# Attention's blocks by head half: score matmuls of two heads on different array rows back to back, and three steps for the value sums in place of five

## The chip, the cores and the metric

The kernel runs on one core of a Trainium2 chip. The metric is device time in microseconds (us), the median of several runs; less is better. The engines are TensorE (PE; PEld is its weight load), VectorE (DVE), ScalarE (ACT), GpSimd (POOL) and SyncE (SP, which issues the loads of weights). Each engine works through its own instructions in order and waits on semaphores for the others.

## The reference, cut to what matters

Two layers of one model, then two layers of a second one (FFN, mixer, FFN), on 512 tokens of width 1024. Only the mixer of the second model is touched, and in it the banded attention: 8 query heads of 64, 2 key/value heads (each serves 4 query heads), 4 blocks of 128 queries, and each block sees itself and its neighbours (2 or 3 blocks of keys).

```python
scores = einsum("bnqkgd,bnskd->bnkgqs", qb, kb) * HEAD_DIM ** -0.5
scores = where(valid, scores, -1e30)              # |q - k| <= 128
m = maximum(max(scores, -1), sink)
p = exp(scores - m);  denom = sum(p, -1) + exp(sink - m)
o = einsum("bnkgqs,bnskd->bnqkgd", p, vb) / denom
```

Beside attention the mixer has a projection of the input (`w_in`), a gated short convolution (3 taps), a wide convolution (31 taps over 2 x 128 channels, with a layer norm behind it), and a projection by `w_out`.

## The kernel before, in words

Each engine has a class (`TensorE`, `VectorE`, `ScalarE`, `Pool`) with one Python generator for each part of the work. A `yield` is a step; `mix(main, side, main_steps, side_steps)` (line 185) lays the steps of two generators beside each other in that ratio, the same way on each engine, so the order of the instructions on an engine is fixed by where the generators yield. In the mixer (`mixer`, TensorE line 1047, VectorE line 1945, ScalarE line 2531) the main generator is `attention` with 80 steps and the side generator is `beside` with 78: one side step is one three-part matmul (`three`, lines 576 to 578: each product of two numbers split in a high and a low half takes three 512-column passes) of the other projections, and for VectorE one tap of the wide convolution (`wide_conv`, line 1234 with `acc`; 60 in all, 16 of them before attention) and, every few steps, the making of a low half of a weight unit (`wlo`), whose high half ScalarE makes (`whi`, line 2161).

`BLOCKS` lists the eight blocks of attention: query block `nb` and key head `kvh`, so that each block holds the four query heads of one key head. I call them B0 to B7. For each block:

- `scores` (TensorE line 1182): for each of four heads one fp32 matmul of 64 rows (the head's 64 numbers) by 256 or 384 keys into one PSUM bank, then a step. The rows are 0 to 63 for key head 0 and 64 to 127 for key head 1, so all four of a block lie on the same rows. VectorE adds the mask and takes the maximum (line 2118) from the bank into `pr`, which frees the bank; behind the fourth come three small operations on `sm`. In the second block of a query block, `turn_ao` turns the finished outputs of the query block before (behind the third head's scores); ScalarE and VectorE copy them out in `copy_ao` and `lower_ao` (`xh`, `xl`).
- `weights` (ScalarE line 2661): four exponentials with row sums, and one of the sink.
- `values` (TensorE line 1193), one block behind the scores: `turned(i)` transposes a head's weights in 2 or 3 pieces of 128 (line 582), ScalarE copies them to `prT` (line 2683, three buffers), and line 1214 multiplies them with the values in pairs of 64-column halves of the array. The order is turned 0 and 1, step, head 0 and turned 2, step, head 1 and turned 3, step, head 2, step, head 3, step. VectorE then divides by the sums (`ao`).

A block thus takes 4 + 1 steps for scores and 5 for values, 80 in all. Scores, turned weights and turned outputs take their PSUM banks in turn from four (`self.ps`), in the last two blocks from three (`self.ps3`); a bank is taken again only when the engine that reads it is done. Elsewhere too matmuls use part of the array's rows: `grams` (line 996) issues four 64-row matmuls that go in turn to rows 0 to 63 and 64 to 127, each pair in two banks (line 1002).

Of the kernel before, what the change touches and what calls it, by code (L numbers as in the profile page):

```python
# [11 lines left out]
ALU = mybir.AluOpType  # L12
# [363 lines left out]
SIDE = (337, 321)  # L376
LEVELS = tuple(enumerate((2, 4, 8, 16, 32, 64)))
OUT_ROWS = (0, 768, 256, 512)
BLOCKS = tuple((nb, kvh, max(nb - 1, 0), min(nb + 2, 4) - max(nb - 1, 0)) for nb in range(4) for kvh in range(2))


class Lane:
# [153 lines left out]
class TensorE(Lane):  # L536
# [510 lines left out]
    def mixer(self, l):  # L1047
        k = self.k
        st = ("mix", l)
        self.at(st)  # L1050
        units = [self.coming("w_in_2", (l,), tuple((256 * u + 128 * j, 768 + 64 * h, 64) for j in range(2) for h in QHEADS))
                 for u in range(4)]
        for t, u in ((2 * tp + t, 2 * up + u) for tp in range(2) for up in range(2) for t in range(2) for u in range(2)):
            wh, wl, i = units[u]
            bank = k.bank(("q", l, t)) if u else self.bank(self.all4, ("q", l, t))
            self.wait_ge(("hi", i), ("lo", i), ("hh", st, t, u // 2), ("hl", st, t, u // 2))
            for j in range(2):
                d = 2 * u + j
                x = slice(512 * d + 128 * t, 512 * d + 128 * t + 128)
                a = self.three(bank[:, :], k.hh[:, x], k.hl[:, x], HALF(wh, j), HALF(wl, j), d == 0, d == 7)  # L1060
            a.then_inc(*self.up(*([("used", i)] if t == 3 else []), *([("q", l, t)] if u == 3 else [])))
            if t < 2 and (t, u) in ((1, 1), (1, 2)):
                self.to_hT_tile(st, 1 + u)
            elif t == 3 and u in (1, 3):
                self.turn_q(l, u // 2)
        for n, _ in enumerate(self.conv_pair(l, 0), 1):
            if n % 8 == 0:
                self.turn_q(l, 1 + n // 8)
        units = [self.coming("w_in_2", (l,), tuple((512 * u + 128 * j, 1280, 256) for j in range(4))) for u in range(2)]
        for t in range(4):  # L1070
# [12 lines left out]
        side = self.beside(l)  # L1083
        for n in range(6):
            next(side)
            if n % 3 == 2:
                self.turn_k(l, n // 3)
        self.at(("pj", st))
        mix(self.attention(l), side, 80, 78)
        drain(side)  # L1090
        keys = [("pj", st, 1, t) for t in range(4)]
        for n, _ in enumerate(self.tiles(keys, "w_out_2", (l,), OUT_ROWS, 512, k.xh8, k.xl8, lambda d: (), self.last4, 4)):
            if n in (9, 11):
                self.to_hT_tile(("ffn2", l), n // 11, self.spare4)
        self.all4.n = 0
# [83 lines left out]
        self.wait_ge(("aon", l, nb, 1))  # L1179
        self.turn(bank, [k.ao[:, i * 128:(i + 1) * 128] for i in range(4)], ("aot", l, nb))  # L1180

    def scores(self, l, nb, kvh, k0, nk):
        k = self.k
        for i in range(4):
            h, q = 4 * kvh + i, 64 * kvh
            bank = self.bank(self.rows_rota, ("as", l, nb, h))
            self.wait_ge(("qT", l, nb), ("kT", l, (k0 + nk - 1) // 2))
            self.e.matmul(bank[:, 0:nk * 128], k.qT[q:q + 64, i * 512 + nb * 128:i * 512 + (nb + 1) * 128],  # L1188
                          k.kT[q:q + 64, k0 * 128:(k0 + nk) * 128], start=True, stop=True).then_inc(*self.up(("as", l, nb, h)))
            if i == 2 and kvh and nb:  # L1190
                self.turn_ao(l, nb - 1)
            yield

    def values(self, l, nb, kvh, k0, nk):
        k = self.k
        at = (l, nb, kvh)
        n0 = 4 * (2 * nb + kvh)
        out = self.bank(self.ao1, ("ao", at))

        def turned(i):  # L1200
# [5 lines left out]
        turned(0)  # L1206
        turned(1)
        yield
        for i in range(4):
            h = 4 * kvh + i  # L1210
            pT = k.prT[(n0 + i) % 3]
            self.wait_ge(("aT", at, i), ("vv", l, (k0 + nk - 1) // 2))
            for j, r in itertools.product(range(nk), (0, 64)):
                t = self.e.matmul(out[r:r + 64, h * 64:(h + 1) * 64], pT[:, j * 128 + r:j * 128 + r + 64],  # L1214
                                  k.v2[:, (k0 + j) * 128 + kvh * 64:(k0 + j) * 128 + kvh * 64 + 64], start=j == 0,
                                  stop=j == nk - 1, skip_group_check=True)
            t.then_inc(*(self.up(("av", at, i), ("ao", at)) if i == 3 else self.up(("av", at, i))))
            if i < 2:
                turned(i + 2)
            yield  # L1220


class VectorE(Lane):
# [721 lines left out]
    def mixer(self, l):  # L1945
# [23 lines left out]
        side = self.beside(l)  # L1969
# [1 line left out]
            next(side)  # L1971
        self.at(("pj", st))
        self.paced = True
        mix(self.attention(l), side, 80, 78)
        drain(side)
        self.paced = False
        self.project(4, st, ("ffn2", l), ALPHA, "ln2", 1e-5, self.held)
# [129 lines left out]
        self.lower(v8(k.xl8), k.bank(key)[:, :].rearrange("p (j n) -> p j n", j=4), v8(k.xh8), [("xah", l, nb)],  # L2107
                   [("free", key)] + ([("xl", l, j) for j in range(2, 6)] if nb == 3 else []))

    def scores(self, l, nb, kvh, k0, nk):  # L2110
        k = self.k
        n0 = 4 * (2 * nb + kvh)
        mo = (k0 - nb + 1) * 128
        s = k.sm[(2 * nb + kvh) % 2]
        for i in range(4):
            key = ("as", l, nb, 4 * kvh + i)
            self.wait_ge(key, ("amask", l), *([("at", (l, nb - 1, kvh), 3)] if nb else []))
            self.e.tensor_tensor_reduce(k.pr[(n0 + i) % 8][:, 0:nk * 128], k.bank(key)[:, 0:nk * 128], k.amask[:, mo:mo + nk * 128],
                                        1.0, -3e38, ALU.add, ALU.max, s[:, i:i + 1]).then_inc(*self.up(("free", key)))
            yield  # L2120
        sk = k.sink[:, 4 * kvh:4 * kvh + 4]
        self.wait_ge(("sink", l))
        self.stt(s[:, 0:4], s[:, 0:4], 0.125, sk, ALU.mult, ALU.max).then_inc(*self.up())
        self.wait_ge()
        self.ts(s[:, 4:8], s[:, 0:4], -1.0, None, ALU.mult).then_inc(*self.up())
        self.wait_ge()
        self.tt(s[:, 8:12], sk, s[:, 0:4], ALU.subtract).then_inc(*self.up(("asm", (l, nb, kvh))))

    def weights(self, l, nb, kvh, k0, nk):
        s = self.k.sm[(2 * nb + kvh) % 2]  # L2130
        self.wait_ge(("ape", (l, nb, kvh)))
# [4 lines left out]
    def values(self, l, nb, kvh, k0, nk):  # L2136
        k = self.k
        at = (l, nb, kvh)
        s = k.sm[(2 * nb + kvh) % 2]
        for i in range(5):  # L2140
            if i == 3:
                self.weights(l, nb, kvh, k0, nk)
            yield
        o = slice(kvh * 256, kvh * 256 + 256)
        self.wait_ge(("ao", at), *([("aot", l, nb - 1)] if nb and kvh == 0 else []))
        self.tt(k.ao[:, o].rearrange("p (h n) -> p h n", h=4), k.bank(("ao", at))[:, o].rearrange("p (h n) -> p h n", h=4),
                s[:, 16:20].unsqueeze(2).broadcast_to([128, 4, 64]), ALU.mult).then_inc(
            *self.up(("aon", l, nb, kvh), ("free", ("ao", at))))


class ScalarE(Lane):
# [379 lines left out]
    def mixer(self, l):  # L2531
# [26 lines left out]
        side = self.beside(l)  # L2558
# [3 lines left out]
                self.turned_k(l, n // 3)  # L2562
        self.at(("pj", st))
        self.paced = True
        mix(self.attention(l), side, 80, 78)
        drain(side)
        self.paced = False
        self.project(4, st, ("ffn2", l), self.held)
# [69 lines left out]
    def attention(self, l):  # L2638
        held = None
        for at in BLOCKS:  # L2640
            for _ in range(4):
                yield
            if at[1] and at[0]:
                self.copy_ao(l, at[0] - 1)
# [16 lines left out]
    def weights(self, l, nb, kvh, k0, nk):  # L2661
        k = self.k
        at = (l, nb, kvh)
        n0 = 4 * (2 * nb + kvh)
        s = k.sm[(2 * nb + kvh) % 2]
        self.wait_ge(("asm", at))
        for i in range(4):
            x = k.pr[(n0 + i) % 8][:, 0:nk * 128]
# [2 lines left out]
        self.wait_ge()  # L2671
        self.act(s[:, 8:12], s[:, 8:12], ACT.Exp).then_inc(*self.up(("ape", at)))

    def values(self, l, nb, kvh, k0, nk):
        k = self.k
        at = (l, nb, kvh)
        n0 = 4 * (2 * nb + kvh)

        def turned(i):
            g, u = divmod(n0 + i - 3, 4)  # L2680
# [5 lines left out]
        turned(0)  # L2686
        turned(1)
        yield
        for i in range(4):
            if i < 2:  # L2690
                turned(i + 2)
            yield


class Pool(Lane):
# [272 lines left out]
```

## Time and profile before

| | us |
|---|---|
| median of 3 runs | 3395.89 (3393.03 to 3396.45) |
| the profiled execution | 3399.57 |
| its span, first to last instruction | 3397.8 |
| PE busy in the span | 3248.0 (96%) |
| DVE busy | 1725.3 (51%) |
| ACT busy | 1097.9 (32%) |
| POOL busy | 155.7 (5%) |
| mean granted TensorE clock | 0.988 |

The span is what the profile's rows add up to; the execution's own time has 1.8 us around it. A busy PE is not PE at its peak, as matmuls overlap: what a group of matmuls costs is read from the starts of the rows around it. Attention of the first layer lies from 1913 to 2042 us, that of the second from 2865 to 2995 us.

### The profile page before, as it was taken

The page shows a single profiled execution, that of the slowest core. Times are in us where ns is not written, and L with a number is a line of the kernel's source. Part 1 is how long each engine was busy: PE and PEld are TensorE (multiplying, and loading weights), DVE is VectorE, ACT ScalarE, POOL GpSimd, SP SyncE. Part 2 cuts the span into 40 slices and gives each one's busy share as a digit, 9 for nine tenths or more (in the row PEclk, how much of TensorE's full clock was granted, in tenths as well). Part 3 has the DMA queues.
Part 4 walks back from the last instruction along what each step waited for, and adds up shares of the span by engine and source line. Part 5 has one row for each costly group of instructions (what it writes and reads, how often), then busy time and mean ns, then how long its engine had stood idle before and what let it go on. Part 6 is the DMA issues. An engine that isn't in the chain of part 4 may idle for free. (4 is left out here: it accounts for less than half of the span.)

```text
span 3397.8 us, 52042 instructions
## 1 busy us (share of the span) xinstructions
PE 3248.0 (96%) x21576; PEld 2552.2 (75%) x21576; DVE 1725.3 (51%) x2526; ACT 1097.9 (32%) x1615; POOL 155.7 (5%) x204
## 2 busy tenths in 40 slices
PE   6999899989999999999999999999999999999998
PEld 5776666767776677788888658888888886588887
DVE  6655654456546644553325866333433347763324
ACT  4342233324433333332322343232233223433321
POOL 1000100000000000000001000000000000000000
PEclk9999899999999999999999999999999999999999
DMA  6222122222222111222232212223222322122232
GB/s 230 76 87 98 67 75 88 94 85 94 88 82 73 63 45 58 97 96 99 95 110 93 81 38 87 99 93 112 87 100 97 109 80 100 39 80 93 100 112 75
DMA packets 83531, 303.74 MB, mean 89 GB/s; under 512 B 9680, under 2 KB 9952, under 8 KB 83296
## 3 DMA queue, kind: packets, MB, share of 16 engines
q1 hardware_dynamic: 78064, 283.11, 23.7%
q0 software_dynamic: 5232, 17.31, 1.5%
q8 instruction: 170, 2.79, 0.3%
q14 instruction: 65, 0.53, 0.0%
HBM read 295.66 MB, written 4.72 MB: 88 GB/s over the span
## 5 line engine op out<-in xcount | busy, mean ns | idle before, releaser
L576 PE MATMUL bank<-hh,whi 128*128 128x512 f32 (+1 forms) x2704 | 1075.9, 398 | 27.3 <-DVE hl L1228 9.5
L578 PE MATMUL bank<-hh,wlo 128*128 128x512 f32 (+1 forms) x2704 | 1027.6, 380 | 0.0
L577 PE MATMUL bank<-hl,whi 128*128 128x512 f32 (+1 forms) x2704 | 1027.2, 380 | 0.0
L1228 DVE TENSOR_TENSOR wlo<-raw,whi 128x1024 fp32r<-128x1024 f32 x498 | 610.5, 1226 | 730.4 <-ACT whi L2161 681.2
L2161 ACT CAST whi<-raw 128x1024 fp32r<-128x1024 f32 x498 | 523.6, 1051 | 733.7 <-PE bank L578 668.2
L576 PEld LDWEIGHTS bank<-hh,whi 128*128 128x128 f32 x2704 | 512.8, 190 | 167.1 <-issue 50.5
L578 PEld LDWEIGHTS bank<-hh,wlo 128*128 128x128 f32 x2704 | 513.0, 190 | 97.7
L577 PEld LDWEIGHTS bank<-hl,whi 128*128 128x128 f32 x2704 | 514.3, 190 | 80.6 <-issue 2.5
L576 PE MATMUL bank<-whi,fh 128*128 128x512 f32 x704 | 274.4, 390 | 0.0
L578 PE MATMUL bank<-whi,fl 128*128 128x512 f32 x704 | 273.9, 389 | 0.0
L577 PE MATMUL bank<-wlo,fh 128*128 128x512 f32 x704 | 273.9, 389 | 0.0
L1228 DVE TENSOR_TENSOR tmp<-tmp,bank 128x512 f32<-128x512 f32 x104 | 71.6, 688 | 240.5 <-PE bank L578 238.1
L2510 ACT CAST fh<-tmp 128x512 fp32r<-128x512 f32 x88 | 54.5, 619 | 374.9 <-DVE tmp L1228 374.9
L578 PEld LDWEIGHTS bank<-whi,fl 128*128 128x128 f32 x704 | 132.1, 188 | 27.6
L577 PEld LDWEIGHTS bank<-wlo,fh 128*128 128x128 f32 x704 | 132.2, 188 | 27.2
L576 PEld LDWEIGHTS bank<-whi,fh 128*128 128x128 f32 x704 | 132.1, 188 | 27.2
L1228 DVE TENSOR_TENSOR fl<-tmp,fh 128x512 fp32r<-128x512 f32 x88 | 61.0, 694 | 71.3 <-ACT fh L2510 71.3
L2429 ACT COPY X<-bank 128x256 f32<-128x256 f32 x96 | 35.8, 373 | 178.1 <-PE bank L582 177.2
L1234 DVE SCALAR_TENSOR_TENSOR acc<-ccp,cols,acc 128x512 f32<-128x512 f32 x120 | 90.2, 752 | 4.3
L576 PE MATMUL bank<-oh,whi 128*128 128x512 f32 x192 | 81.8, 426 | 7.9 <-DVE ogs L1228 7.9
L2156 ACT ACTIVATE tmp<-bank 128x512 f32<-128x512 f32 x120 | 72.0, 600 | 52.0 <-PE bank L578 48.8
L1757 DVE COPY_PREDICATED U<-lmask,bank 128x256 f32<-128x256 uint32 x64 | 32.7, 510 | 99.4 <-PE bank L902 94.1
(325 smaller groups left out, 3488.7 us busy)
## 6 DMA issues: line engine op xcount, KB each, us to landing
raw<-in_W SPq DMA_DIRECT2D x514, 512.0 KB, 3.2
bc<-in_ln_g POOLq DMA_DIRECT2D x6, 512.0 KB, 4.2
bc<-in_ln_b POOLq DMA_DIRECT2D x6, 512.0 KB, 5.8
xn<-in_x SPq DMA_DIRECT2D x4, 512.0 KB, 9.1
mrg<-in_W SPq DMA_DIRECT2D x2, 1024.0 KB, 13.0
AR<-in_W SPq DMA_DIRECT2D x2, 1024.0 KB, 18.4
xn<-in_x POOLq DMA_DIRECT2D x4, 512.0 KB, 4.9
xd<-xn POOLq DMA_DIRECT2D x4, 512.0 KB, 3.5
```

Source lines behind the costliest of these rows:

```text
L576: e.matmul(out, ah, bh, start=first, stop=False, skip_group_check=True)
L577: e.matmul(out, ah, bl, start=False, stop=False, skip_group_check=True)
L578: return e.matmul(out, al, bh, start=False, stop=last, skip_group_check=True)
L1228: return self.e.tensor_tensor(o, a, b, op)
L1234: return self.e.scalar_tensor_tensor(out=o, in0=a, scalar=s, in1=b, op0=op0, op1=op1)
L1757: e.copy_predicated(FOUR_PART(U, 1, n), m, TIGHT(wb, n)).then_inc(*self.up(("cu", at, lv + 1), ("free", ("cw", at, lv))))
L2156: return self.e.activation(o, a, f, bias=bias, scale=scale, **kw)
L2161: self.e.copy(self.k.halves(i)[0], self.k.raw_unit(n)).then_inc(*self.up(("hi", i)))
L2429: self.e.copy(TIGHT(X, n), FOUR_PART(k.bank(key), 0, n)).then_inc(*self.up(("cx", at, lv), ("free", key)))
L2510: self.e.copy(HALF(k.fh, m), tm).then_inc(*self.up(("fh", st, m)))
```

## The change

The two key heads share a block now, and two heads of each make up its four: block half 0 has heads 0, 4, 1, 5 and half 1 has heads 2, 6, 3, 7. Neighbours in this order lie on rows 0 to 63 and 64 to 127. Scores yield once for two heads; in `values`, heads 0 and 1 follow each other, then turned 2 and 3, a step, heads 2 and 3, a step. So a block takes 2 + 1 steps for scores and 3 for values, 48 in all, and `mix` lays 78 side steps beside 48. `turn_ao` comes behind the fourth head's scores. The views of VectorE's small operations and of `ao` follow the new order of heads.

```diff
-BLOCKS = tuple((nb, kvh, max(nb - 1, 0), min(nb + 2, 4) - max(nb - 1, 0)) for nb in range(4) for kvh in range(2))
+BLOCKS = tuple((nb, half, max(nb - 1, 0), min(nb + 2, 4) - max(nb - 1, 0)) for nb in range(4) for half in range(2))
+HEADS = tuple(tuple((a, v, 4 * v + a) for a in (2 * half, 2 * half + 1) for v in range(2)) for half in range(2))
+BY_HALF = lambda x, half: x.rearrange("p (v a n) -> p a v n", v=2, a=4)[:, 2 * half:2 * half + 2, :, :]
+BY_PAIR = lambda x: x.rearrange("p (a v) -> p a v", v=2)
...
-        mix(self.attention(l), side, 80, 78)
+        mix(self.attention(l), side, 48, 78)
...
     (TensorE)
-    def scores(self, l, nb, kvh, k0, nk):
-        for i in range(4):
-            h, q = 4 * kvh + i, 64 * kvh
+    def scores(self, l, nb, half, k0, nk):
+        for i, (a, v, h) in enumerate(HEADS[half]):
+            q = 64 * v
             bank = self.bank(self.rows_rota, ("as", l, nb, h))
...
-            if i == 2 and kvh and nb:
+            if i == 3 and half and nb:
                 self.turn_ao(l, nb - 1)
-            yield
+            if i % 2:
+                yield
...
-        for i in range(4):
-            h = 4 * kvh + i
+        for i, (_, v, h) in enumerate(HEADS[half]):
             pT = k.prT[(n0 + i) % 3]
             self.wait_ge(("aT", at, i), ("vv", l, (k0 + nk - 1) // 2))
             for j, r in itertools.product(range(nk), (0, 64)):
...
-            if i < 2:
-                turned(i + 2)
-            yield
+            if i == 1:
+                turned(2)
+                turned(3)
+            if i % 2:
+                yield
...
     (VectorE)
+            if i % 2:
+                yield
-        sk = k.sink[:, 4 * kvh:4 * kvh + 4]
+        sk = k.sink[:, :].rearrange("p (v a) -> p a v", v=2)[:, 2 * half:2 * half + 2, :]
...
-        for i in range(5):
-            if i == 3:
-                self.weights(l, nb, kvh, k0, nk)
+        for i in range(3):
+            if i == 2:
+                self.weights(l, nb, half, k0, nk)
             yield
...
-        self.tt(k.ao[:, o].rearrange("p (h n) -> p h n", h=4), k.bank(("ao", at))[:, o].rearrange("p (h n) -> p h n", h=4),
-                s[:, 16:20].unsqueeze(2).broadcast_to([128, 4, 64]), ALU.mult).then_inc(
+        self.tt(BY_HALF(k.ao[:, :], half), BY_HALF(k.bank(("ao", at))[:, :], half),
+                BY_PAIR(s[:, 16:20]).unsqueeze(3).broadcast_to([128, 2, 2, 64]), ALU.mult).then_inc(
...
     (ScalarE, attention)
-            for _ in range(4):
+            for _ in range(2):
                 yield
...
     (ScalarE, values)
-        for i in range(4):
-            if i < 2:
-                turned(i + 2)
-            yield
+        turned(2)
+        turned(3)
+        yield
+        yield
```

## Rows read from the trace of the kernel before

**Rows 1.** Stretches of attention: length, busy of each engine (instructions), PEclk, DMA, GB/s.
```profile
1913.00:1966.80 53.80, 49.06 (x249) 28.59 (x249) 50.60 (x102) 21.39 (x50) 1.06 (x2) 0.94 0.19 65
1966.80:1985.10 18.30, 18.00 (x129) 11.23 (x128) 14.09 (x29) 7.65 (x17) 0.00 (x0) 0.99 0.08 30
1985.10:2042.40 57.30, 53.76 (x349) 33.10 (x347) 29.07 (x66) 31.28 (x67) 0.00 (x0) 1.00 0.10 38
1961.00:1967.00 6.00, 5.27 (x28) 3.65 (x30) 5.53 (x9) 1.73 (x5) 0.00 (x0) 0.50 0.07 29
```

**Rows 2.** Waits in 1913 to 2043 (PE), 1913 to 1985 (DVE): total, times, longest.
```profile
PE bank L582 <- DVE xl L1228: 5.6, 3, 3.9
...
DVE ao L1228 <- PE bank L1214: 2.9, 2, 2.3
DVE tz L1228 <- PE bank L578: 0.5, 1, 0.5
```

**Rows 3.** PE by time: its longest wait's end; then a head's scores, 384 keys.
```profile
1961.73 0.47 PE L582 MATMUL bank<-ident,pr 128*128 128x128 f32 x1 [3.86 <-DVE xl L1228]
...
1970.17 0.40 PE L578 MATMUL bank<-hh,wlo 128*128 128x512 f32 x1
1970.49 0.91 PE L1188 MATMUL bank<-kT,qT 64*128 64x384 f32 x2
1971.33 0.50 PE L576 MATMUL bank<-hh,whi 128*128 128x512 f32 x1
1971.67 0.40 PE L577 MATMUL bank<-hl,whi 128*128 128x512 f32 x1
1971.90 0.40 PE L578 MATMUL bank<-hh,wlo 128*128 128x512 f32 x1
```

**Rows 4.** The same around scores of 256 keys.
```profile
1915.82 0.40 PE L578 MATMUL bank<-hh,wlo 128*128 128x512 f32 x1
1916.14 0.70 PE L1188 MATMUL bank<-kT,qT 64*128 64x256 f32 x2
1916.77 0.50 PE L576 MATMUL bank<-hh,whi 128*128 128x512 f32 x1
1917.11 0.39 PE L577 MATMUL bank<-hl,whi 128*128 128x512 f32 x1
```

**Rows 5.** PE at line 1002, four matmuls in turn on both halves of the rows.
```profile
270.30 0.49 PE L1002 MATMUL bank<-AR,KH 64*128 64x256 f32 x2
...
270.30 1.14 PE L1002 MATMUL bank<-AR,KH 64*128 64x256 f32 x8
271.36 0.50 PE L576 MATMUL bank<-whi,hh 128*128 128x512 f32 x1
```

**Rows 6.** PE, value sums: head with turned weights; head alone; a head of two key blocks.
```profile
1979.80 0.40 PE L578 MATMUL bank<-hh,wlo 128*128 128x512 f32 x1
...
1981.24 0.40 PE L577 MATMUL bank<-hl,whi 128*128 128x512 f32 x1
...
1982.87 0.39 PE L578 MATMUL bank<-hh,wlo 128*128 128x512 f32 x1
1983.19 0.57 PE L1214 MATMUL bank<-v,prT 128*64 128x64 f32 x12
1984.03 0.40 PE L577 MATMUL bank<-hl,whi 128*128 128x512 f32 x1
...
2040.89 0.45 PE L1214 MATMUL bank<-v,prT 128*64 128x64 f32 x8
```

**Rows 7.** DVE in order of time: the last tap, and what follows it.
```profile
1984.34 0.75 DVE L1234 SCALAR_TENSOR_TENSOR acc<-ccp,cols,acc 128x512 f32<-128x512 f32 x1
1986.35 0.56 DVE L2118 CUSTOM_DVE_ANT_0 pr<-bank,amask 128x384 f32<-128x384 f32 x1 [1.26 <-PE bank L1188]
```

**Rows 8.** ACT in order of time, B5's last copies to B6's first.
```profile
2016.63 0.99 ACT L2683 COPY prT<-bank 128x384 f32<-128x384 f32 x2
2027.55 0.37 ACT L2683 COPY prT<-bank 128x256 f32<-128x256 f32 x1
```

More of the change, by code:

```diff
@@ L1180, in turn_ao, with values @@
         self.turn(bank, [k.ao[:, i * 128:(i + 1) * 128] for i in range(4)], ("aot", l, nb))
-    def scores(self, l, nb, kvh, k0, nk):
+    def scores(self, l, nb, half, k0, nk):
         k = self.k
-        for i in range(4):
-            h, q = 4 * kvh + i, 64 * kvh
+        for i, (a, v, h) in enumerate(HEADS[half]):
+            q = 64 * v
             bank = self.bank(self.rows_rota, ("as", l, nb, h))
             self.wait_ge(("qT", l, nb), ("kT", l, (k0 + nk - 1) // 2))
-            self.e.matmul(bank[:, 0:nk * 128], k.qT[q:q + 64, i * 512 + nb * 128:i * 512 + (nb + 1) * 128],
+            self.e.matmul(bank[:, 0:nk * 128], k.qT[q:q + 64, a * 512 + nb * 128:a * 512 + (nb + 1) * 128],
                           k.kT[q:q + 64, k0 * 128:(k0 + nk) * 128], start=True, stop=True).then_inc(*self.up(("as", l, nb, h)))
-            if i == 2 and kvh and nb:
+            if i == 3 and half and nb:
                 self.turn_ao(l, nb - 1)
-            yield
-    def values(self, l, nb, kvh, k0, nk):
+            if i % 2:
+                yield
+    def values(self, l, nb, half, k0, nk):
         k = self.k
-        at = (l, nb, kvh)
-        n0 = 4 * (2 * nb + kvh)
+        at = (l, nb, half)
+        n0 = 4 * (2 * nb + half)
         out = self.bank(self.ao1, ("ao", at))
@@ L1214, in values @@
                 t = self.e.matmul(out[r:r + 64, h * 64:(h + 1) * 64], pT[:, j * 128 + r:j * 128 + r + 64],
-                                  k.v2[:, (k0 + j) * 128 + kvh * 64:(k0 + j) * 128 + kvh * 64 + 64], start=j == 0,
+                                  k.v2[:, (k0 + j) * 128 + v * 64:(k0 + j) * 128 + v * 64 + 64], start=j == 0,
                                   stop=j == nk - 1, skip_group_check=True)
             t.then_inc(*(self.up(("av", at, i), ("ao", at)) if i == 3 else self.up(("av", at, i))))
-            if i < 2:
-                turned(i + 2)
-            yield
+            if i == 1:
[3 more added lines that the diff above has]
+                yield
 class VectorE(Lane):
@@ L1973, in mixer @@
         self.paced = True
-        mix(self.attention(l), side, 80, 78)
+        mix(self.attention(l), side, 48, 78)
         drain(side)
@@ L2108, in lower_ao, with scores @@
                    [("free", key)] + ([("xl", l, j) for j in range(2, 6)] if nb == 3 else []))
-    def scores(self, l, nb, kvh, k0, nk):
+    def scores(self, l, nb, half, k0, nk):
         k = self.k
-        n0 = 4 * (2 * nb + kvh)
+        n0 = 4 * (2 * nb + half)
         mo = (k0 - nb + 1) * 128
-        s = k.sm[(2 * nb + kvh) % 2]
-        for i in range(4):
-            key = ("as", l, nb, 4 * kvh + i)
-            self.wait_ge(key, ("amask", l), *([("at", (l, nb - 1, kvh), 3)] if nb else []))
+        s = k.sm[(2 * nb + half) % 2]
+        for i, (_, _, h) in enumerate(HEADS[half]):
+            key = ("as", l, nb, h)
+            self.wait_ge(key, ("amask", l), *([("at", (l, nb - 1, half), 3)] if nb else []))
             self.e.tensor_tensor_reduce(k.pr[(n0 + i) % 8][:, 0:nk * 128], k.bank(key)[:, 0:nk * 128], k.amask[:, mo:mo + nk * 128],
                                         1.0, -3e38, ALU.add, ALU.max, s[:, i:i + 1]).then_inc(*self.up(("free", key)))
-            yield
-        sk = k.sink[:, 4 * kvh:4 * kvh + 4]
+            if i % 2:
+                yield
+        sk = k.sink[:, :].rearrange("p (v a) -> p a v", v=2)[:, 2 * half:2 * half + 2, :]
         self.wait_ge(("sink", l))
-        self.stt(s[:, 0:4], s[:, 0:4], 0.125, sk, ALU.mult, ALU.max).then_inc(*self.up())
+        self.stt(BY_PAIR(s[:, 0:4]), BY_PAIR(s[:, 0:4]), 0.125, sk, ALU.mult, ALU.max).then_inc(*self.up())
         self.wait_ge()
@@ L2126, in scores, with weights @@
         self.wait_ge()
[L2127 to L2131, printed above, removed]
+        self.tt(BY_PAIR(s[:, 8:12]), sk, BY_PAIR(s[:, 0:4]), ALU.subtract).then_inc(*self.up(("asm", (l, nb, half))))
+    def weights(self, l, nb, half, k0, nk):
+        s = self.k.sm[(2 * nb + half) % 2]
+        self.wait_ge(("ape", (l, nb, half)))
         self.tt(s[:, 8:12], s[:, 8:12], s[:, 12:16], ALU.add).then_inc(*self.up())
@@ L2134, in weights, with values @@
         self.e.reciprocal(s[:, 16:20], s[:, 8:12]).then_inc(*self.up())
-    def values(self, l, nb, kvh, k0, nk):
+    def values(self, l, nb, half, k0, nk):
         k = self.k
-        at = (l, nb, kvh)
-        s = k.sm[(2 * nb + kvh) % 2]
-        for i in range(5):
-            if i == 3:
-                self.weights(l, nb, kvh, k0, nk)
-            yield
-        o = slice(kvh * 256, kvh * 256 + 256)
-        self.wait_ge(("ao", at), *([("aot", l, nb - 1)] if nb and kvh == 0 else []))
-        self.tt(k.ao[:, o].rearrange("p (h n) -> p h n", h=4), k.bank(("ao", at))[:, o].rearrange("p (h n) -> p h n", h=4),
-                s[:, 16:20].unsqueeze(2).broadcast_to([128, 4, 64]), ALU.mult).then_inc(
-            *self.up(("aon", l, nb, kvh), ("free", ("ao", at))))
+        at = (l, nb, half)
+        s = k.sm[(2 * nb + half) % 2]
+        for i in range(3):
+            if i == 2:
+                self.weights(l, nb, half, k0, nk)
+            yield
+        self.wait_ge(("ao", at), *([("aot", l, nb - 1)] if nb and half == 0 else []))
+        self.tt(BY_HALF(k.ao[:, :], half), BY_HALF(k.bank(("ao", at))[:, :], half),
+                BY_PAIR(s[:, 16:20]).unsqueeze(3).broadcast_to([128, 2, 2, 64]), ALU.mult).then_inc(
+            *self.up(("aon", l, nb, half), ("free", ("ao", at))))
 class ScalarE(Lane):
@@ L2564, in mixer @@
         self.paced = True
-        mix(self.attention(l), side, 80, 78)
+        mix(self.attention(l), side, 48, 78)
         drain(side)
@@ L2659, in copy_ao, with weights @@
             *self.up(("xah", l, nb), *([("xh", l, j) for j in range(2, 6)] if nb == 3 else [])))
-    def weights(self, l, nb, kvh, k0, nk):
+    def weights(self, l, nb, half, k0, nk):
         k = self.k
-        at = (l, nb, kvh)
-        n0 = 4 * (2 * nb + kvh)
-        s = k.sm[(2 * nb + kvh) % 2]
+        at = (l, nb, half)
+        n0 = 4 * (2 * nb + half)
+        s = k.sm[(2 * nb + half) % 2]
         self.wait_ge(("asm", at))
@@ L2672, in weights, with values @@
         self.act(s[:, 8:12], s[:, 8:12], ACT.Exp).then_inc(*self.up(("ape", at)))
-    def values(self, l, nb, kvh, k0, nk):
+    def values(self, l, nb, half, k0, nk):
         k = self.k
-        at = (l, nb, kvh)
-        n0 = 4 * (2 * nb + kvh)
+        at = (l, nb, half)
+        n0 = 4 * (2 * nb + half)
         def turned(i):
@@ L2688, in values @@
         yield
-        for i in range(4):
-            if i < 2:
-                turned(i + 2)
-            yield
+        turned(2)
+        turned(3)
+        yield
+        yield
 class Pool(Lane):
```

## The prediction, made before the change was run

> **What bounds the kernel now.** I read the page first: PE is busy for 96% of the span, DVE for half of it. So what shortens PE shortens the kernel, unless another engine holds PE up in that stretch. Next the table of stretches over attention in the first layer, where the change lies, since the average over the span says nothing about it [rows 1]. The second layer shows the same picture 952 us later, with the same waits to 0.3 us, so I work out one layer and double it. The reader is to see three things.
>
> First, from 1913 to 1966.8 us DVE is busy for 50.60 of 53.80 us with 102 instructions; the 3.2 us left are 0.03 us between one and the next, and no wait of DVE falls in it. DVE is full there: PE hands it scores, and it has the taps of the wide convolution besides. PE is idle for 4.7 us in the same stretch. Second, from 1966.8 to 1985.1, where the last tap ends [rows 7], DVE waits for 3.4 us in all, 2.9 of it for the value sums and 0.5 for a bank of the short convolution [rows 2]. Those 2.9 us come from PE's own wait of 3.9 us for a bank that DVE frees in `lower_ao` (`xl`), after which PE ran at a granted clock of 0.50 (1.2 GHz) for 6 us [rows 1 to 3]. Third, from 1985.1 to 2042.4 PE is busy for 53.76 of 57.30 us and DVE for 29.07: PE is the bound, with 3.5 us of gaps.
>
> **Scores.** A full pass of 512 columns starts 0.23 us after the one before (1971.67 to 1971.90) [rows 3]. From the pass ahead of a head's scores to the second pass behind them it takes 1.50 us with 384 keys; two passes would take 0.46, so these scores cost 1.04 us, of which 0.84 is from their start to the next start. With 256 keys it is 1.29 - 0.46 = 0.83, with 0.63 from start to start [rows 4]. The difference of the starts, 0.21 us for 128 keys, gives 0.42 us for the streaming of 256 keys, and the rest is a fixed cost at each change from full matmuls to these and back. The old code lays a side step between any two heads, so each head pays it.
>
> Do two heads on different rows really run at the same time? Line 1002 answers it in this trace: four matmuls of 64 rows by 256 columns, in turn on the upper and the lower rows, two banks. The first passes of the first two start together (two are there within 0.02 us), and the four take 1.06 us to the next start [rows 5]. One after another they would take 0.63 + 3 x 0.42 = 1.89; as two pairs side by side 0.63 + 0.42 = 1.05. The new score pairs have the same form: rows 0 to 63 and 64 to 127, each into its own bank. So a pair costs what a head cost, and one of each two heads is free: 16 pairs in a layer, 8 with 384 keys and 8 with 256, 8 x 1.04 + 8 x 0.83 = 15.0 us of PE. The bounds: nothing side by side leaves the fixed cost saved, about 0.2 us a pair (1.04 - 0.84), 3.2 us; above 15.0 I see nothing.
>
> **Value sums.** A head alone costs 1.16 - 0.46 = 0.70 us; with turned weights behind it 1.44 - 0.46 = 0.98 [rows 6]. Its 12 matmuls show 0.57 us against 0.45 for 8, which is 0.06 us for each pair of halves, so a head directly behind another adds 6 x 0.06 = 0.36 in place of 0.70. The change joins heads 0 and 1, and 2 and 3: 2 x 0.34 = 0.68 us a block, 5.4 us in 8 blocks. The lower bound is 0.2 a joint (entry 0.09 and exit 0.11 against 0.23), 3.2 us. Turned 2 and 3 together save nothing I can see: three pieces alone cost 0.28 behind a head and stream for longer than they wait.
>
> Together PE loses 20.4 us of work in a layer. What of it reaches the end differs by stretch.
>
> **Stretch one, to the last tap.** The 78 side steps stay, and the last tap (the 44th of attention's side steps) still falls behind B4: 45 x 78/80 before, 27 x 78/48 after. In it PE saves 4 x 0.83 + 6 x 1.04 + 4 x 0.68 = 12.3 us, but DVE's work is the same: the same reductions, the same taps, small operations of the same 4 columns in another view, the same 256 elements of `ao` (0.42 us each; a few hundredths either way at most). DVE can only lose its 3.4 us of waits. Will it? PE gets further ahead, stops sooner for banks, and is at hand when DVE frees one. The one wait that matters is again for `xl`, now before turned 3 only, as `turn_ao` comes one bank later. Behind it PE owes turned 3, two joined heads, three groups of side steps (4.9 x 0.69) and one pair of scores, some 5.7 us, before DVE runs dry: released at 1961.73 [rows 3], PE had DVE at work until 1966.8 [rows 1], 5.1 us, to which come `ao` (0.4), 1.6 taps at 0.75 [rows 7] and one multiply (0.7), 7.4 us. At the full clock that covers it. But PE will again have stood for some 4 us, and if the clock falls again for 6 us [rows 1] the 5.7 become 8.7 and DVE waits 1.3. I take 2.5 of the 3.4 us, with bounds 0 and 4.7 (the 1.3 us more if PE is already past the scores for which DVE waits right behind the last tap [rows 7]).
>
> **Stretch two, PE bound.** Here PE saves two pairs at 1.04 and four at 0.83, 5.4 us, and four blocks of value sums, 2.7: 8.1 us. Against it stand two new waits. ACT has no gap from its copies for B5 to the end of the first copy for B6, 2017.62 to 2027.92, 10.3 us (table loads, the wide convolution's SiLU, four exponentials, a cast) [rows 8]. PE's way between the value sums on both sides was 11.8 us and will be 1.06 + 5 x 1.625 x 0.69 + 2 x 0.83 + about 0.9 for the turns = 9.2 us, so it waits about 1.1 us. And in B6 and B7, with three banks, the second pair's second score needs the bank of the first, and turned 0 and 1 come right after two scores in place of one; for these I put 1.0 us, an estimate between 0 and 4 (each of the four turns behind DVE's 0.4 us reductions plus one low half of a unit). Head 1 now waits for its copy directly behind head 0, with turned 2 and 3 queued behind; PE comes there 1.6 side steps after the turn in place of one, so I count nothing (bound 0.3 a block, 1.2 us). Stretch two gives 6.0 us, bounds 3 and 8.1.
>
> The loads and the halving of weights keep their order and place by side step; no DMA moves past another.
>
> **Sum.** 2 x (2.5 + 6.0) = 17 us. The profiled execution took 3399.57, 1.8 over its span, so the changed one is expected at 3382.6. The median of the three runs lies 3.7 lower: 3395.9 - 17 = 3379.
>
> **The rivals.** *DVE takes the whole first stretch.* Nothing comes from it, and only 2 x 6.0 = 12 us are left: 3384. For it: DVE is full for 54 us, and PE's stop for `xl` stays. Against: DVE did wait, and for a PE that now has less to do. The Trainium skill (TensorEngine Tiling (Array Packing), PSUM Bottleneck) says that tiling speeds up TensorE but not the evacuation of PSUM, which may become the bottleneck; the trace has that state already in stretch one and not in stretch two, and by the rule alone this rival would hold.
>
> *The pairs don't overlap.* Then only joints are saved, 0.2 x 6 + 2.7 in stretch two less 1 for waits, and 2 in stretch one: 2 x 4.9, about 3386. Against it stands line 1002.
>
> *All PE work counts.* 2 x 20.4 = 41 us, 3355. Against it a DVE that can't be shortened below 68.7 us in stretch one.
>
> *The other side: the clock.* PE will stand for some 14 us in stretch one of each layer where it stood for 4.7, and each spell of 6 us at 1.2 GHz takes 3 us of PE's work. A spell behind which DVE still has work costs nothing; one that reaches the end of stretch one or lies in stretch two costs its 3 us. It decides from six such spells more in the two layers, which eat the 17 us; with eight the time would be 3395.9 + 7 = 3403. For it: the fall after the 3.9 us wait in both layers. Against: the many shorter waits in the stretch brought no fall. The skill (TensorE: Matmul & The Clock Gate, What's actually happening) states that the throttled clock is the default and that activity releases it; the trace agrees as far as that one wait goes.
>
> **How the numbers follow.** My forecast holds with 0.60, DVE taking all with 0.18, no overlap 0.07, all of PE's work 0.03, the clock 0.05, and 0.07 for waits that leave between 0 and 6 us. The low end takes 4.0 of stretch one's 4.7, the whole 8.1, and 1.4 of stretch two's old gaps of 3.5, which joined steps may close: 2 x 13.5, 3369; the high end 2 x 3 us: 3390. A measurement tells a difference from about 0.2%, 6.8 us, so the same is 3389.1 to 3402.7: faster 0.86, same 0.09, slower 0.05.
>
> **What would show it.** Right: at line 1188 four matmul records start in two pairs within some 0.01 us, and 0.84 us from the first to the next full pass; attention's length, 129.3 us from 1913 to the last `turn_ao`, falls to about 121; DVE has under 2 us of waits to the last tap, and PE some 14 us of idle time there. Wrong: score records of a pair that follow each other by 0.4 us or more; DVE waits of over 3 us in stretch one; a PEclk under 0.9 in stretch two; or PE gaps over 6 us in stretch two, which would put the loss on ScalarE's chain or the three banks.

## The result, and the profile after

The changed kernel takes 3370.57 us (median of 4 runs, 3367.75 to 3373.48) against 3396.17 of the kernel before, measured beside it: ratio 0.9924, 95% interval 0.9909 to 0.9940. On another chip it took 3369.93 against 3397.89, ratio 0.9920 (0.9907 to 0.9934). So the change gives 26 to 28 us where I had forecast 17. The time is within the stated range, near its low end, and some of that is luck: two terms of the sum were too small, as the last part shows, and a kernel without any overlap of heads (E3) took nearly the same time.

The profiled execution took 3367.75 with a span of 3365.9, 31.9 us under the span before. Not all of that belongs to the change: attention begins 4.5 us earlier, at 1908.6, though all code ahead of it is the same. Part of the cause is where the clock fell in those stages: ahead of attention TensorE stood at 1.2 GHz for 51.2 us in this trace and for 58.0 in that of the kernel before, which accounts for at most 3.4 of the 4.5 us; the rest is open. Attention itself, from the first scores to the last `turn_ao`, takes 115.9 us in place of 129.2, the same in both layers: 13.3 us twice. Line numbers have moved: scores are line 1191, value sums 1217, transposes 585, `sm` 2123, and a side step's three passes are 579 to 581.

First the price list. Rows of PE around a pair of scores of 384 keys. The first line counts only the matmuls that start before 1959.70, which are the first passes of the two heads; they start 0.007 us apart. The other lines give the pair whole, in order of time:

```profile
1959.32 0.59 PE L1191 MATMUL bank<-kT,qT 64*128 64x384 f32 x2
...
1959.00 0.39 PE L581 MATMUL bank<-hh,wlo 128*128 128x512 f32 x1
1959.32 0.92 PE L1191 MATMUL bank<-kT,qT 64*128 64x384 f32 x4
1960.16 0.50 PE L579 MATMUL bank<-hh,whi 128*128 128x512 f32 x1
1960.50 0.39 PE L580 MATMUL bank<-hl,whi 128*128 128x512 f32 x1
```

The reader is to compare with [rows 3]: two heads take 0.84 us from start to next start, as one did, and 1960.50 - 1959.00 - 0.46 = 1.04 us with entry and exit. Both signs that I had named for this are there: the four passes of a pair start in two pairs within 0.01 us, and the next full pass starts 0.84 us after the first. A joined pair of value sums with three key blocks costs 1.05 us (forecast 1.06), and with the turned weights behind it 1.66 (0.98 twice before).

Next the stretches. I cut at the first mean matmul of the wide convolution (line 1152, now 1155), which waits for the last tap; the columns are those of [rows 1]. Before:

```profile
1913.10:1988.70 75.60, 70.67 (x387) 41.60 (x388) 66.82 (x134) 31.99 (x74) 1.06 (x2) 0.95 0.16 53
1988.70:2042.40 53.70, 50.16 (x338) 31.33 (x336) 26.84 (x63) 28.24 (x58) 0.00 (x0) 1.00 0.11 40
```

After:

```profile
1908.60:1977.30 68.70, 58.06 (x386) 38.25 (x386) 64.57 (x130) 32.01 (x74) 1.06 (x2) 0.98 0.17 58
1977.30:2024.50 47.20, 44.83 (x337) 31.69 (x337) 29.08 (x66) 28.25 (x58) 0.00 (x0) 0.96 0.13 46
```

VectorE has no wait at all left before the last tap, and PE is idle for 10.6 of 68.7 us. The two rows that decide are PE's at the mean matmul and VectorE's at the last tap:

```profile
1977.33 1.98 PE L1155 MATMUL bank<-acc,mean 128*128 128x512 f32 x4 [1.58 <-DVE acc L1239]
```

```profile
1976.52 0.75 DVE L1239 SCALAR_TENSOR_TENSOR acc<-ccp,cols,acc 128x512 f32<-128x512 f32 x1
```

Before, PE came to this matmul 3.6 us after the last tap had ended (1988.67 against 1985.09). Now it stands there 1.6 us ahead of it. PE's waits after the change, from 1908 to 1978, then from 1977 to 2025 (total, times, longest):

```profile
PE bank L585 <- DVE sm L2123: 4.9, 3, 2.4
PE bank L585 <- ACT pr L2161: 2.3, 1, 2.3
PE bank L1155 <- DVE acc L1239: 1.6, 1, 1.6
PE bank L585 <- DVE xl L1233: 1.3, 1, 1.3
...
PE bank L1217 <- ACT prT L2688: 2.3, 1, 2.3
```

### The profile page after: what moved, and what is told of

It is laid out like the page before. It is cut to its first block and busy times, and to the rows that moved or that the text cites. A ratio compares the mean times of both kernels' runs of the same rounds, so it can differ in the third digit from the quotient of the medians.

```text
span 3365.9 us, 52046 instructions
## 1 busy us (share of the span) xinstructions
PE 3209.7 (95%) x21576; PEld 2544.7 (76%) x21576; DVE 1724.8 (51%) x2526; ACT 1098.0 (33%) x1615; POOL 155.8 (5%) x204
## 5 line engine op out<-in xcount | busy, mean ns | idle before, releaser
L2515 ACT CAST fh<-tmp 128x512 fp32r<-128x512 f32 x88 | 54.5, 619 | 375.2 <-DVE tmp L1233 375.2
```

The costliest lines, as they stand in the source:

```text
L2515: self.e.copy(HALF(k.fh, m), tm).then_inc(*self.up(("fh", st, m)))
```

## The experiments

All timed runs stand beside the kernel before on their own chip. For the traces I give attention's two parts, from the first scores to the mean matmul and from there to the last `turn_ao`; before they are 75.5 and 53.7 us, after 68.7 and 47.1. The parts hold the same work in all kernels but E1, E2, E6 and E9, where the mean matmul stands at another place between the blocks.

**E1, pairs of scores, but the sums in five steps.**

```diff
-        mix(self.attention(l), side, 48, 78)
+        mix(self.attention(l), side, 64, 78)
...
-            if i == 1:
-                turned(2)
-                turned(3)
-            if i % 2:
-                yield
+            if i < 2:
+                turned(i + 2)
+            yield
```

> The changed blocks with scores in pairs on different rows, but the value sums in the old five steps (64 steps of attention beside 78). Theory, PE ahead at the last tap: VectorE's floor of 68.7 us to the last tap stays, and PE reaches the mean matmul of the wide convolution right behind it, 6.8 us earlier than before; behind it only the pairs count, 1 x 1.04 + 4 x 0.83 = 4.4 us. So 11.2 us a layer less about 0.5 of waits: 21 us faster than before, 5 slower than the changed kernel. Rival, the coarser steps themselves gave what the forecast missed: the surplus of the change (26 measured against 17) goes with the steps, and this gives about 12 to 14 us. Rival, all PE work counts: 30 us.

Measured: 3379.76 against 3396.07, ratio 0.9950 (0.9938 to 0.9963), 16 us faster. Parts: 73.1 and 50.1 us in the first layer, 70.5 and 49.2 in the second. The median lies between the first two expectations, and the interval, 13 to 21 us, rules out neither. VectorE's floor of 68.7 does not hold for this order: the last tap and the mean matmul come behind one more pair of scores, so VectorE has two more reductions ahead of its last tap, at 0.6 us each. In the second layer, where it has no wait, it needs 69.9 us to the last tap; in the first it needs 71.6, with 1.8 us of waits for PE. PE was held once for 2.6 us in this part, in both layers, for copies of ScalarE, which had stood itself for a product of VectorE, with a cast still to do. PE, then ScalarE:

```profile
1964.99 0.91 PE L1217 MATMUL bank<-v,prT 128*64 128x64 f32 x12 [2.60 <-ACT prT L2686]
```

```profile
1962.69 0.62 ACT L2620 CAST xh<-tz 128x512 fp32r<-128x512 f32 x1 [7.60 <-DVE tz L1231]
1963.38 1.04 ACT L2164 CAST whi<-raw 128x1024 fp32r<-128x1024 f32 x1
1964.46 0.99 ACT L2686 COPY prT<-bank 128x384 f32<-128x384 f32 x2
```

The clock fell to 1.2 GHz at this wait for 6.8 us, and once more for as long in the second part of that layer. The layers run the same code, yet attention is 6.0 us shorter than before in the first and 9.6 in the second. At 1.2 GHz TensorE stood for 17.1 us of the first and 10.2 of the second, and at half speed the 6.8 us between them are 3.4 us of work, about the size of the difference.

**E2, old blocks and scores, sums in three steps.** The edit is the change's own in `values` on all three engines, with `mix(..., 64, 78)`.

> The old blocks (four heads of one key group) and old scores with a step each, with only the value sums in three steps (64 steps of attention beside 78). Theory: the joints of heads save 0.68 us a block; 2.7 us come in stretch two, and in stretch one between 2.7 and 4 us, since PE gets some of the way ahead of VectorE: 5.4 to 6.7 us a layer, 11 to 13 us in all. Rival, coarser steps gave the surplus: 14 us or more. Rival, the sums wait for ScalarE's copies and save nothing: under 5 us.

Measured: 3391.25 against 3396.07, ratio 0.9988 (0.9979 to 0.9997), 5 us faster, less than I expected (the interval is 1 to 7 us), and within the last rival's "under 5 us". In the traces attention is 2.4 and 4.3 us shorter. Its first parts take 71.4 and 69.9 us, its second 55.5 and 54.9; but here scores of two heads, 2.1 us of PE, lie behind the mean matmul that lay ahead of it before. Set right by that, the first parts gain 2.1 and 3.5 us, and the second only 0.3 and 0.8 of the 2.7 that their joints save. PE's waits in the second part of the first layer, 4.1 us where there were 3.5 before:

```profile
PE bank L582 <- DVE xl L1230: 2.0, 1, 2.0
PE bank L1214 <- ACT prT L2685: 1.8, 1, 1.8
PE bank L582 <- DVE sm L2120: 0.3, 1, 0.3
```

With 64 steps each step has 1.22 side steps beside it in place of 1.6. The sums have then 3.7 side steps to cover their copies, and before they had 4.9. That this is the cause is argued from the waits and not shown; I did not vary the ratio alone. E1 and E2 together give 21 us, and the whole change 26 to 28: the parts do not simply add, as each comes with its own mix.

**E3, the new steps with the old blocks: no two scores side by side.** The kernel before, with

```diff
-        mix(self.attention(l), side, 80, 78)
+        mix(self.attention(l), side, 48, 78)
...
-            if i == 2 and kvh and nb:
+            if i == 3 and kvh and nb:
                 self.turn_ao(l, nb - 1)
-            yield
+            if i % 2:
+                yield
```

and the sums in three steps.

> The changed steps (48 beside 78), scores two after each other and sums in three steps, but the old blocks: all four heads of a block lie on the same rows, so no two scores can run side by side. Theory: a joined pair of scores saves only its 0.2 us of entry and exit, so 16 x 0.2 + 5.4 = 8.6 us of PE a layer in place of 20.4; of it 1 + 2.7 us behind the mean matmul, and 4 to 6.8 ahead of it: 8 to 10 us a layer, 16 to 20 us faster than before and 7 to 10 slower than the changed kernel. The score records of a pair start 0.4 us and more apart. Rival, the rows don't matter: the same time as the changed kernel, 26 us faster than before.

Measured: 3372.15 against 3396.07, ratio 0.9929 (0.9917 to 0.9942), 24 us faster. I was wrong by 4 to 8 us, and the rival had the time right: without any overlap the kernel is as fast as the changed one, within what the intervals tell. But the rows do matter to PE. A pair in this kernel:

```profile
1961.68 0.39 PE L578 MATMUL bank<-hh,wlo 128*128 128x512 f32 x1
1962.00 1.55 PE L1188 MATMUL bank<-kT,qT 64*128 64x384 f32 x4
1963.49 0.50 PE L576 MATMUL bank<-hh,whi 128*128 128x512 f32 x1
1963.82 0.40 PE L577 MATMUL bank<-hl,whi 128*128 128x512 f32 x1
```

It costs 1963.82 - 1961.68 - 0.46 = 1.68 us against 1.04. Overlap is worth 0.64 us a pair, and 0.41 with 256 keys. And joining two scores without overlap saves 2 x 1.04 - 1.68 = 0.40 us, twice what I had put. The parts say where overlap went: the first takes 68.7 us here too, the floor of VectorE, with PE busy for more of it. The second is 1.1 us longer than in the changed kernel in the first layer, and 1.6 in the second, of the 2.3 us that overlap is worth there (one pair at 0.64, four at 0.41):

```profile
1911.30:1980.00 68.70, 63.08 (x386) 41.19 (x386) 64.56 (x131) 32.01 (x74) 1.06 (x2) 1.00 0.18 59
1980.00:2028.20 48.20, 45.63 (x335) 32.49 (x336) 29.06 (x66) 28.24 (x58) 0.00 (x0) 1.00 0.14 45
```

**E4, E5 and E7, VectorE relieved.** In each kernel every second tap is left out, so that the wide convolution is not computed in full:

```diff
             for w in range(1, 31):
-                self.wait_ge()
-                self.stt(ac, cp[:, j, w:w + 512], ...
+                if w % 2 == 0:
+                    self.wait_ge()
+                    self.stt(ac, cp[:, j, w:w + 512], ...
                 yield
```

E4 is the kernel before with that edit, E5 the changed one, E7 the kernel of E3.

> The kernel before without every second tap of the wide convolution (30 of its 60 three-operand instructions on VectorE a layer; that part of the output is left out). The step order is unchanged, so only VectorE's load falls, by 22 x 0.79 = 17 us a layer in stretch one. Theory: before the change PE lost to VectorE only its 4.7 us of waits there and some 3 us of half clock behind them; without them attention takes about 122 us in place of 129: 12 to 16 us faster than the kernel before. Rival, VectorE's load is no bound: no change.

> The changed kernel without the same taps. Theory: with VectorE's floor gone PE's 20.4 us of saved work a layer count nearly whole, less about 3 us for copies of ScalarE: attention takes 104 to 106 us, and the time is 33 to 37 us below that of the kernel before with half taps. Rival, banks and ScalarE's chain bound stretch one of the changed kernel as much as VectorE's amount of work does: 20 to 27 us below, as with all taps.

> The new steps with four heads of one key group in a block (no two scores side by side), without the same taps. Overlap itself is worth 1.68 - 1.05 = 0.63 us a pair with 384 keys and 1.25 - 0.84 = 0.41 with 256, 8.3 us of PE a layer. Theory: with VectorE's floor gone these count: 14 to 17 us slower than the changed kernel with half taps. Rival, overlap is off the path in any case (the two kernels with all taps differed by under 2 us): within 4 us of it.

Measured on one chip, beside 3397.89 of the kernel before:

| | us | ratio to before (95%) | parts of attention, first layer |
|---|---|---|---|
| E4, before | 3382.84 | 0.9956 (0.9944 to 0.9969) | 69.5 + 53.7 |
| E5, after | 3339.88 | 0.9832 (0.9819 to 0.9846) | 54.5 + 47.1 |
| E7, same rows | 3358.18 | 0.9883 (0.9870 to 0.9897) | 60.7 + 48.8 |

E4 is 15 us faster than before, as expected. E5 lies 43.0 us below E4 (21.6 a layer in the traces): all of PE's 40.8 us of saved work count once VectorE is no bound, and two more, as its waits are shorter too, 2.8 us in the first layer against 5.8. E7 lies 18.3 us above E5, against 2 x 8.3 of overlap priced from the rows and 14 to 17 expected; in the traces attention differs by 7.9 and 7.3 us, so 3 of the 18.3 lie outside attention or between executions. The first parts of E5 and E7 show PE without a gap:

```profile
1911.70:1966.20 54.50, 54.46 (x386) 37.66 (x387) 46.93 (x109) 30.77 (x70) 1.06 (x2) 1.00 0.21 73
```

```profile
1911.50:1972.20 60.70, 60.69 (x387) 41.64 (x388) 47.55 (x110) 31.38 (x72) 1.06 (x2) 1.00 0.20 65
```

So the rival of banks and ScalarE's chain is out for stretch one: nothing but VectorE's amount of work holds the changed kernel there. For stretch two it is not: E5's second part takes 47.1 us, the same as with all taps. In E4 and E5 I left out the same 30 instructions, so the difference between them is the change's own; that the relief is worth 30 us to the changed kernel (3369.93 to 3339.88) and 15 to the one before shows how much more the changed kernel leans on VectorE.

**The changed kernel again.**

> The changed kernel once more, on the chip of these runs. 0.9924 of the kernel before, 24 to 28 us faster; attention 115.9 us in both layers unless the clock falls at other places.

Measured: 3369.93, ratio 0.9920 (0.9907 to 0.9934), attention 115.9 us in both layers.

**E6, taps spread over 54 side steps in place of 50.**

```diff
-            want = min(10 + m, 60) + sum(m >= x for x in self.norm_steps)
+            want = min(10 + m * 50 // 54, 60) + sum(m >= x for x in self.norm_steps)
-    norm_steps = (52, 58)                      # TensorE
+    norm_steps = (56, 61)
-    norm_steps = (54, 60, 63, 64, 66, 71)      # VectorE
+    norm_steps = (58, 63, 65, 66, 68, 72)
-    norm_steps = (55, 61, 68)                  # ScalarE
+    norm_steps = (59, 64, 70)
```

> The changed kernel with the wide convolution's 50 taps of the side steps spread over 54 of them in place of 50, and the mean, variance and norm behind them 1 to 4 side steps later (they still end before the output projection wants them). Theory: VectorE is the floor up to the last tap, while PE stands for some 10 us; with the last tap 4 side steps later, PE has done 4 x 0.69 = 2.8 us more when the taps end, and nothing of VectorE's own work grows, so 2 to 2.8 us a layer, 4 to 5.5 us faster than the changed kernel, 30 us faster than before. Rival, PE is bound in stretch one by the banks and not by VectorE's amount of work: no change against the changed kernel, or slower by what the squeezed norm makes the output projection wait.

> The changed kernel with its taps spread over 54 side steps once more, on the chip of the two above, since its gain over the changed kernel (4.3 us of attention in the trace) is near what a measurement can tell. 0.9905 to 0.992 of the kernel before; attention 113.7 us in both layers.

Measured: 3366.93 against 3396.07, ratio 0.9913 (0.9899 to 0.9926), and again 3366.27 against 3397.01, ratio 0.9912 (0.9899 to 0.9926). The medians lie 3 to 4 us below those of the changed kernel, and the traces say 115.9 - 113.7 = 2.2 us of attention in each of both layers, the same in two executions. That is the size that the theory gave, but the trace does not show its path: PE still stands for 10.0 us in the first part (10.6 before this edit), and what went is most of its wait for ScalarE's copies, 2.6 to 0.9 us in the layer, and the fall of the clock behind it. The edit moves taps and norm together, and I did not separate them. As the intervals of the ratios overlap, the trace carries this claim more than the times do. It is the fastest full kernel of the study. Its parts:

```profile
1913.20:1988.10 74.90, 64.91 (x443) 43.48 (x444) 69.27 (x143) 34.48 (x79) 1.06 (x2) 0.98 0.18 61
1988.10:2027.00 38.90, 37.38 (x282) 25.92 (x280) 24.33 (x53) 27.05 (x55) 0.00 (x0) 1.00 0.12 41
```

**E8, low halves on GpSimd, and E9, both edits.** Within attention VectorE leaves out the subtraction for `wlo`, and GpSimd does it:

```diff
     def halve(self, i, n):                      # VectorE
+        if self.lend is not None:
+            self.lend.append((i, n))
+            return
...
+        for i, n in k.lent[l]:                  # Pool, mixer
+            hi, lo = k.halves(i)
+            self.wait_raw(n)
+            self.wait_ge(("hi", i), *([("used", i - RING)] if i >= RING else []))
+            self.e.tensor_tensor(lo, k.raw_unit(n), hi.bitcast(F32), ALU.subtract).then_inc(*self.up(("lo", i)))
```

> The changed kernel with the low halves of the weight units that fall into attention made by GpSimd in place of VectorE (one subtraction of 1024 columns each, 1.23 us on VectorE, five of them in stretch one). Theory: VectorE's floor to the last tap falls by 5 x 1.26 = 6.3 us, PE stands for 10 us there now, so 5 to 6 us a layer, 10 to 12 us faster than the changed kernel, if GpSimd makes each half in under the 5.5 us that a unit's eight side steps take. Rival, GpSimd is slow or holds VectorE up: PE waits for the low halves, and the time is that of the changed kernel or worse.

> Both edits: the taps spread over 54 side steps and the low halves on GpSimd. Theory: PE's 10 us of waits in stretch one fall to 2 or less; 5 to 8 us a layer, 10 to 16 us faster than the changed kernel, so about 3357. Rival, GpSimd as above: no faster than the spread taps alone, 3366.

Measured: E8 3380.52, ratio 0.9955 (0.9942 to 0.9967), some 10 us slower than the changed kernel; E9 3371.18, ratio 0.9928 (0.9914 to 0.9941), 5 slower than E6. The rival holds by VectorE being held up; PE does not wait for the low halves. A GpSimd subtraction and VectorE at the same time, in E8:

```profile
1945.63 2.86 POOL L2865 TENSOR_TENSOR wlo<-raw,whi 128x1024 fp32r<-128x1024 f32 x1 [8.51 <-PE bank L586]
```

```profile
1945.49 0.75 DVE L1241 SCALAR_TENSOR_TENSOR acc<-ccp,cols,acc 128x512 f32<-128x512 f32 x1
1946.28 2.23 DVE L1241 SCALAR_TENSOR_TENSOR sm<-sm,sink 128x4 f32<-128x4 f32 x1
1948.54 0.17 DVE L1238 TENSOR_SCALAR sm<-sm 128x4 f32<-128x4 f32 x1
```

An operation on four columns takes 2.23 us in place of 0.16 and ends 0.02 us behind GpSimd's. The taps from 1908 to 1985 come to 0.90 us in the mean, 0.75 without GpSimd:

```profile
L1241 DVE SCALAR_TENSOR_TENSOR acc<-ccp,cols,acc 128x512 f32<-128x512 f32 x52 | 46.8, 901 | 1.9
L1241 DVE SCALAR_TENSOR_TENSOR sm<-sm,sink 128x4 f32<-128x4 f32 x5 | 2.9, 578 | 0.2
```

52 x 0.15 + 5 x 0.42 = 9.9 us are lost where five halves of 1.23 us are saved, and the first part grows from 68.7 to 73.0. The Trainium skill states it (SBUF — State Buffer, SBUF: two separate sides): the ports that VectorE and GpSimd share are an exclusive lock for a whole instruction, also against a VectorE operation with two SBUF inputs. The trace agrees in both forms seen here, and with the `sm` operation to 0.02 us.

## Why the prediction was right, and where it was short

**Prices.** Right, nearly to the hundredth: pair 1.04, joined sums 1.05, 0.6 to 0.7 a block at the joints. That line 1002 already had the answer on overlap holds. One bound was wrong: I took the fixed cost of scores as 1.04 - 0.84 = 0.20 us, but the 0.84 from start to next start holds another 0.2 besides its 0.64 of streaming. E3's rows give 0.40. In the rival without overlap it would have made 16 x 0.2 = 3.2 us more PE work saved in a layer, which takes that rival from 3386 to 3380 at most. E3 was 24 us faster than before, and 3380 is 16: what is still missing is the handover below, which that rival left out as my forecast did.

**Stretch one's floor.** Right: with this order and all its work VectorE needs 68.7 us to the last tap; 68.65 and 68.67 were measured in the two layers of the changed kernel, 68.64 and 68.66 in E3, with no wait of VectorE in either. I had taken 2.5 of the 3.4 us (3.3 came), for fear of the clock behind the wait for `xl`. That wait was 1.3 us this time, as PE had lost time in earlier waits (for `sm` and `pr`), and the clock did not fall there.

**The handover.** This is the term that was mis-sized most. A layer gave 13.3 us where I had 8.5, and of the 4.8 between them about 2.5 are the handover, 1.4 the balance of waits in stretch two, and 0.8 the waits of VectorE that I had kept. I split the gain at the last tap and gave stretch two only PE's savings behind it, 8.1 us less 2.0 for new waits; 10.0 was measured (57.2 to 47.2). The split assumed that PE stands at the same place of its own program when the taps end, the start of B5. But PE, with 12 us less to do in front of a fixed floor, gets ahead until its own next need of VectorE stops it, and that is not B5 but the mean matmul, 3.4 us of PE's work further on (1985.29 to 1988.67 before). Cut at the mean matmul, the sum closes: 75.5 - 68.7 = 6.8 us, which is VectorE's 3.4 us of waits and PE's 3.4, and behind it 6.5 of the 7.1 us of PE work saved (1.04 + 4 x 0.83 + 2.7). My 8.1 for stretch two had only one pair, 1.04 us, of these 3.4. My upper bound for stretch one had 1.3 of these 3.4 us. E5 and E7, where the floor is away, give the whole of PE's work, and E3 shows the same 68.7 with less saved.

**New waits in stretch two.** I put 2.0 us. ScalarE's copies hold PE for 2.3 us at B5, where the kernel before had 1.2 and where I had looked for nothing; behind this wait the clock was at 1.2 GHz for 3.4 us. The three banks cost nothing. But the old waits of 3.5 us went too (1.7 for `xl`, 1.2 for `prT`, 0.6 for `ao`), so the balance is about nothing.

The 1.1 us that I had put on ScalarE's chain to B6 are there, though the changed kernel's waits do not show them. ScalarE again has no gap from B5's last copies to B6's first, which ends at 2013.29, and PE starts B6's value sums at 2013.36: the slow clock had brought PE there just too late to wait. E5 shows both cases, as the clock fell in the second part of its first layer (PEclk 0.96) and not in that of its second:

```profile
1966.20:2013.30 47.10, 44.75 (x337) 31.55 (x336) 27.95 (x62) 29.64 (x63) 0.00 (x0) 0.96 0.14 46
2887.10:2934.20 47.10, 43.58 (x337) 30.70 (x336) 27.96 (x62) 29.63 (x63) 0.00 (x0) 1.00 0.14 46
```

```profile
2923.07 0.86 PE L1217 MATMUL bank<-v,prT 128*64 128x64 f32 x16 [1.17 <-ACT prT L2689]
```

At the full clock PE waits 1.2 us at B6, and both parts take 47.1 us. So in E5 stretch two follows ScalarE's copies up to B6 and the fall of the clock there costs nothing; with all taps the part takes 47.1 us as well.

**The rivals.** VectorE does take stretch one, but only from the point where its waits are gone, which the 3384 of that rival left out. The clock as the other side did not come: PE stands for 10.6 us in the first part in many short waits, with one half-clock spell of 3.4 us there and one behind it, against one of 6.8 before, and all of the first falls where VectorE has work in hand; the one behind is hidden by ScalarE's chain. PEclk in stretch two was 0.96 and PE's gap there 2.3 us, both within what I had named; attention's length was 5 us under the 121 I had named, half of it by the handover, and PE's idle time in the first part 10.6 in place of 14, by the handover.

**What overlap is worth.** With the floor in place, 1.6 us between medians of two chips, which is no difference that can be measured (2.7 us of attention in the traces); without it 18.3 us (15.2 of attention in the traces). The headline of the change is overlap of two heads, but nearly all of its time comes with the new steps alone, as E3 shows: they pay the fixed cost of a change of matmul form less often, and VectorE no longer waits. What stays open is how much of E1's and E2's shortfall is the ratio of side steps; in E1's first layer most of it is the clock.

## What to carry to other kernels

When one engine's work shrinks in front of another engine's fixed amount of work, don't cut the sum where the fixed work ends: find the first instruction of the shrinking engine that needs its end, and count all that engine's work up to there as hidden. Then look whether a third engine's chain (here ScalarE's copies) ends last behind it. Price a saving twice, on its own engine and against the floor of the next one; a test that halves the floor's load (E5) tells the two apart in one run. A step split in two costs its fixed entry and exit each time, so joining like matmuls can be worth as much as running them side by side.

## What the runs showed of the hardware that I had not expected

- An isolated fp32 matmul of 64 rows between full passes costs 0.40 us beyond its streaming (1.04 for 0.64), half of it before and behind, and half between its own first start and the next start beyond the streaming; two in a row on the same rows pay it once (1.68 for 1.28 in E3).
- A GpSimd subtraction of 1024 columns with both inputs in SBUF takes 2.3 to 2.9 us (VectorE 1.23), and VectorE's three-operand instructions beside it in E8 ended only with it. Lending VectorE's work to an idle GpSimd made the kernel 10 us slower.
- The clock's falls move between executions in stages whose code is the same: in the two executions of E6 TensorE stood at 1.2 GHz for 58.0 and 61.4 us ahead of attention, which began at 1911.3 and 1913.2 us. Over all executions of this study it began between 1906.4 and 1915.0 us, with edits that reach at most some ten taps ahead of it. Lengths of a stage carry a comparison of a few us better than the span does.
